# One diffusion step with retention, latent attention and experts on one core: fewer retention state updates, value products placed earlier, input norm placed ahead of the modulation weights

## The chip, the cores and the metric

The kernel runs on one core of a Trainium2 chip, as one program. The metric is the device time of one execution in microseconds (us); of several executions the median is taken. All arithmetic is in 32-bit floats. In the profile every product of the program appears as two matmul records of the same shape (a product of 128x128 by 128x512 is two records of 128x512); a transpose is one record.

## What is computed

640 tokens (128 context tokens and 512 latent tokens, 1024 wide) pass through two layers. Layer 0 mixes tokens by retention in two directions, layer 1 by latent attention; after each comes a mixture of 16 experts. Each norm is scaled and shifted by rows computed from a condition vector.

```
m = silu(cond) @ w_ada + b_ada ; sh1, sc1, g1, sh2, sc2, g2 = split(m)
h = rmsnorm(x, norm1) * (1 + sc1) + sh1
# layer 0, per head (4) and direction (forward, backward), chunks of 128 tokens:
att = (q_c @ k_c.T) * intra
o_c = att @ v_c + (q_c * q_dec) @ s
s   = s * c_dec + (k_c * k_dec).T @ v_c
# layer 1:
cq, ckv, kpe = split(h @ w_in) ; ckv = rmsnorm(ckv, kv_norm)
v = ckv @ w_uv          # values of all keys, 8 heads at once
```

The latent tokens are four chunks that start from a given state; the context tokens are one chunk that starts from zero. The states after the context chunk are outputs; the states after the last latent chunk are not. So a direction has four latent chunks; steps 6 to 9 below compute the outputs of the third and the fourth of each.

## The kernel before

Each engine has its own list of instructions, written out by hand in one function per engine; semaphores tie them. Tokens lie in five tiles of 128; tile 4 (`PT`) is the context. PE means TensorE, DVE VectorE, ACT ScalarE, POOL GpSimd, SP the queue that issues most DMAs.

**Start.** SP issues the small vectors (L559 to L565), then four chunks of `w_ada` of 2 MB each (`load_chunk`, L568), then the five tiles of `x` (L583), then the first weights of head 0 (L568 again). PE multiplies the condition by each chunk (`chunk`, L913), ACT copies the result to `stage` (L1563), PE sums four row groups of it (`chunk_sum`, L939), and ACT copies that to `mod` (L1567). `PRE_ORDER` sets the order of these eight steps. Behind the last one DVE forms `a1` from `mod` (`mod_first`, L1870 and L1871); ACT squares each tile of `x` (`square`, L1559), POOL makes the reciprocal root (`rstd`, L798 and L799), DVE multiplies (`normalise`, L1899), PE transposes eight blocks (`norm_T`, L951), and ACT and DVE each evict half of them with scale and shift into `hT` (`norm_evac`, L1594; `h_evac`, L1890). The first product of head 0 is `P1` (L1058), which reads the ACT half of tiles 0 and 1; then the context's own product (L1074).

**A head of layer 0.** Head 0 is written out, heads 1 to 3 are a loop on every engine. PE computes q, k and v by seven block products on sums of blocks, and the scores of the five chunks (L1155). Then follow ten steps (`STEPS`, a pair of tile and direction each): the product of masked scores and values (L1185), for latent tiles two products of the decayed query and the state (L1193), and, from step 2 to step 9, one update of a state out of `STATES`: two products of 128x512 (L1202), after which two transposes (`k_T`, L1168) fetch the keys of the next update. Behind every step one to three products of the gates (`AFTER_STEP`, L1131) and, in some, a slice of the modulation of a later layer (L923) are placed. DVE takes the statistics of the output (L2099, L2101), updates the state (L2109), scales the transposed keys (`k_decay`, L2048), normalises the output (L2115, which frees bank 5 for the next step), and multiplies by gains and gate. POOL makes the reciprocal roots and the decayed queries (`qdec_mul`, L815).

**Latents of layer 1.** PE computes the latents of each tile (`latent`, L1377 and L1379); POOL, DVE and ACT normalise them; `lat_T` (L1361 to L1365) transposes them into banks 2 and 3; ACT and DVE evict. `lat_T(NT)` does the same for the cached keys. The values of six key tiles (L1400), 24 products into banks 4 to 7, begin when all of that has been evicted; ACT and DVE evict them in turn (L1791, L2363). Then the heads of layer 1 follow (`head_proj`, L1414).

## Time and profile before

| | |
|---|---|
| median of 3 runs | 1804.79 us (1801.92 to 1810.95) |
| the profiled execution's own time | 1819.1 us |
| its span, first to last instruction | 1817.3 us |
| PE busy | 1700.9 us, 94% of the span |
| DVE, ACT, POOL busy | 709.3, 260.7, 180.6 us |
| mean granted clock of TensorE | 0.977 of full speed |

A row of the timeline reads: start, duration from first to last of the merged instructions, engine, line, operation, tiles, sizes, count, and in brackets the idle time ahead and what ended it. The profiled execution is 14.3 us above the median of the runs.

### The profile page before, as it was taken

Reading aid. Unit: us, or ns where it says so; the run is one execution under the profiler, and the core shown is the slowest. Engines: PE = TensorE matmul, PEld = TensorE weight load, DVE = VectorE, ACT = ScalarE, POOL = GpSimd, SP = SyncE. Lnnn points to the kernel's source line nnn. Section 1 sums busy time; section 2 is a strip of 40 time slices with the busy share of each in tenths; the row PEclk is TensorE's granted clock in tenths of the full one; section 3 lists DMA queues with packets and bytes.
Section 4 is the critical chain, followed back from the end, with each engine's and each line's share of the span. In section 5 each row is a group of like instructions: output and inputs, shape, how many; then the busy total and the mean of one; then the engine's idle time right before and its main releaser. Section 6 shows DMA issues by size and latency. Waiting matters only on the chain.

```text
span 1817.3 us, 17218 instructions
## 1 busy us (share of the span) xinstructions
PE 1700.9 (94%) x6322; PEld 953.2 (52%) x6322; DVE 709.3 (39%) x1187; ACT 260.7 (14%) x554; POOL 180.6 (10%) x274
## 2 busy tenths in 40 slices
PE   5999989999899999999898999898999989999995
PEld 2764374643756456644454444354666664544442
DVE  1335533366233553346572322322333333523324
ACT  5100000000000000000121111321323221111111
POOL 1000100011000110001001222110000000012222
PEclk9999999999899999999999999998999999999998
DMA  9432552015410163102766999830000023469994
GB/s 339 172 139 93 177 192 90 0 47 204 178 47 0 67 227 133 46 0 92 256 247 203 342 343 346 253 118 0 24 21 6 7 70 140 167 229 342 344 345 145
DMA packets 159369, 281.38 MB, mean 155 GB/s; under 512 B 11428, under 2 KB 106424, under 8 KB 154184
## 3 DMA queue, kind: packets, MB, share of 16 engines
q1 hardware_dynamic: 144616, 236.39, 37.2%
q0 software_dynamic: 9248, 33.61, 6.9%
q10 hardware_dynamic: 5440, 10.49, 1.6%
q8 instruction: 44, 0.72, 0.2%
q14 instruction: 21, 0.17, 0.0%
HBM read 247.09 MB, written 33.37 MB: 154 GB/s over the span
## 4 chain that ended last, share of the span: by engine, by line
PE 79%; SPq 7%; DMA 5%; DVE 4%; issue 2%; ACT 2%; POOL 0%; ACTq 0%; POOLq 0%; DVEq 0%
PE banks L1058 11%; PE banks L1131 11%; PE banks L1033 8%; PE banks L1293 7%; PE banks L1414 4%; PE banks L1513 4%; SPq L646 4%; PE banks L1127 3%; PE banks L1310 3%; PE banks L1202 3%; PE banks L1193 3%; SPq L647 3%; PE banks L1185 2%; PE banks L1445 2%; DMA wr<-in_moe_w_down 2%
## 5 line engine op out<-in xcount | busy, mean ns | idle before, releaser
L1293 PE MATMUL banks<-wr,arena 128*128 128x512 f32 x512 | 231.4, 606 | 9.6 <-DMA wr<-in_moe_w_down 6.8
L1131 PE MATMUL banks<-wr 128*128 128x512 f32 x432 | 191.4, 592 | 0.0
L1058 PE MATMUL banks<-wr 128*128 128x256 f32 x768 | 173.9, 386 | 10.0 <-issue 8.4
L1058 PEld LDWEIGHTS banks<-wr 128*128 128x128 f32 x768 | 148.1, 194 | 34.5 <-issue 12.5
L1293 PEld LDWEIGHTS banks<-wr,arena 128*128 128x128 f32 x512 | 96.6, 194 | 123.3 <-issue 122.2
L1033 PE MATMUL banks<-wr,arena 128*128 128x512 f32 x320 | 143.6, 604 | 2.1 <-ACT arena L1620 2.1
L1131 PEld LDWEIGHTS banks<-wr 128*128 128x128 f32 x432 | 80.0, 190 | 91.2 <-issue 91.2
L1310 PE MATMUL banks<-wr,arena 128*128 128x512 f32 x256 | 115.4, 593 | 0.9 <-ACT arena L1733 0.9
L1033 PEld LDWEIGHTS banks<-wr,arena 128*128 128x128 f32 x320 | 60.5, 194 | 73.5 <-issue 72.5
L861 POOL DMA_INDIRECT acc_dram<-arena,put_ids x30 | 60.5, 2016 | 264.8 <-DVE arena L2269 264.8
L2254 DVE SCALAR_TENSOR_TENSOR arena<-banks,slot_w,arena 128x256 f32<-128x256 f32 x32 | 15.5, 483 | 182.2 <-ACT arena L1729 182.2
L2269 DVE TENSOR_TENSOR arena<-banks,arena 128x1024 f32<-128x1024 f32 x32 | 39.2, 1225 | 83.4 <-PE banks L1310 83.4
L1310 PEld LDWEIGHTS banks<-wr,arena 128*128 128x128 f32 x256 | 46.3, 190 | 48.3 <-issue 46.9
L1513 PE MATMUL banks<-wr,arena 128*128 128x512 f32 x160 | 69.6, 593 | 0.0
L815 POOL TENSOR_TENSOR arena<-arena 128x256 f32<-128x256 f32 x32 | 23.4, 735 | 377.8 <-DVE arena L2020 377.8
L2099 DVE BATCH_NORM_STATS2 st<-banks 128x6 f32<-128x512 f32 x40 | 28.0, 699 | 82.7 <-PE banks L1193 65.7
L1193 PE MATMUL banks<-arena 128*128 128x512 f32 x128 | 60.1, 592 | 0.0
L1202 PE MATMUL banks<-arena 128*128 128x512 f32 x128 | 60.1, 592 | 0.0
L1970 DVE TENSOR_TENSOR arena<-banks,arena 128x512 f32<-128x512 f32 x40 | 27.6, 691 | 82.5 <-PE banks L1033 82.4
L1127 PE MATMUL banks<-wr 128*128 128x512 f32 x128 | 55.7, 593 | 0.0
L1414 PE MATMUL banks<-arena 128*128 128x512 f32 (+1 forms) x192 | 53.3, 434 | 0.8 <-issue 0.8
L1645 ACT ACTIVATE arena<-arena 128x512 f32<-128x512 f32 x24 | 15.1, 629 | 254.9 <-DVE arena L2079 114.1
(310 smaller groups left out, 2165.7 us busy)
## 6 DMA issues: line engine op xcount, KB each, us to landing
wr<-in_w_ada SPq DMA_DIRECT2D x24, 2048.0 KB, 7.6
wr<-in_moe_w_gate SPq DMA_DIRECT2D x32, 1024.0 KB, 13.4
wr<-in_moe_w_up SPq DMA_DIRECT2D x32, 1024.0 KB, 16.3
wr<-in_moe_w_down SPq DMA_DIRECT2D x32, 1024.0 KB, 15.8
wr<-in_ret_w_in SPq DMA_DIRECT2D x12, 2048.0 KB, 15.9
wr<-in_ret_w_in SPq DMA_DIRECT2D x8, 1024.0 KB, 11.1
wr<-in_ret_w_out SPq DMA_DIRECT2D x4, 2048.0 KB, 7.8
arena<-mod_rows_dram SPq DMA_DIRECT2D x14, 512.0 KB, 6.9
```

The costliest lines, as they stand in the source:

```text
L646: sp.dma_start(gu[:, :, 1, :], w_u[l][e]).then_inc(S(f"w_full{b}"), 16)
L861: g.indirect_dma_start(out=acc[l], out_offset=bass.IndirectOffsetOnAxis(ap=put_ids[:, e:e + 1], axis=0), in_=ysb[:, b, :], in_offset=None, ...
L1033: mm = mmul(bank[6 + hf][:], yT[:, t % 2, j, :], ring(slot)[:, j * D + hf * 512:j * D + hf * 512 + 512], start=(j == 0), stop=(j == 3))
L1058: mm = mmul(dst[:, r * 256:r * 256 + 256], lhs, rhs, start=(start and r == 0 and k == 0), stop=(k == 3), skip_group_check=True)
L1127: mm = mmul(dst, hT[:, k, TS:T], ring8(2 + int(tile))[:, k, :], start=(k == 0), stop=(k == KT - 1))
L1131: mm = mmul(dst, X[X_OF[p]][:, k, cols], W[p][:, k, :], start=(k == 0 and p not in ("P2", "P7", "P3")), stop=(k == 3), skip_group_check=True)
L1193: mm = mmul(bank[5][:], qd[:, u % 2, j, :], St[:, r, j, :], start=False, stop=(j == 1))
L1202: mm = mmul(bank[6 + j][:], kd[:, u % 2, tile_cols(j)], vv[:, STATES[u][0], :], start=True, stop=True)
L1293: mm = mmul(bank[2][:], xgT[:, e.par, k, :], expert_w(e.buf)[0][:, k].rearrange("p g f -> p (g f)"), start=(k == 0), stop=(k == KT - 1))
L1310: mm = mmul(bank[4 + 2 * e.par + hf][:], gactT[:, e.par, j, :], expert_w(e.buf)[1][:, j, hf * 512:hf * 512 + 512], start=(j == 0), stop=(j ...
L1414: mm = mmul(dst, lhs(k), rhs(k), start=(k == 0), stop=(k == nk - 1))
L1513: mm = mmul(bank[4 + hf][:], oTb[:, t % 2, k, :], w_o[:, k, hf * 512:hf * 512 + 512], start=(k == 0), stop=(k == KT - 1))
```

## The change

Three things are changed.

First, each head updates six states instead of eight. `STATES` loses `(3, 0)` and `(1, 1)`. After steps 6 and 7, where these stood, PE now multiplies the keys of that chunk by the queries of the chunk that comes after it (`DIRECT`), DVE scales the scores by both decays into `attm`, and in steps 8 and 9 one more product of these scores and the values stands in for the missing update. The older state is used there, so POOL multiplies the query a second time, by the decay of a chunk.

Second, in layer 1 the values are computed tile by tile by `values(kt)`, the first two ahead of the transposes of the cached keys and of the last latents, in banks 6, 7, 0 and 1; DVE evicts latents 3 before it works on latents 4.

Third, at the start `x` is loaded ahead of the four chunks, its squares stand ahead of the chunk copies on ACT and its first four multiplications ahead of `mod` on DVE. The chunks are taken in the order 0, 2, 1, 3, so that half of the scale and shift (`mod_half`) is there after two of them. The transposes are spread between the chunks, and some small products without a use (`idle_products`) are added on PE.

```diff
-STATES = [(0, 0), (2, 1), (1, 0), (3, 1), (3, 0), (1, 1), (4, 0), (4, 1)]
+STATES = [(0, 0), (2, 1), (1, 0), (3, 1), (4, 0), (4, 1)]
+STATE_AT = {2: 0, 3: 1, 4: 2, 5: 3, 8: 4, 9: 5}
+STATE_FOR = {4: 0, 5: 1, 6: 2, 7: 3, 8: 2, 9: 3}
+DIRECT = {6: (0, 2, 3, 0), 7: (1, 0, 1, 2)}
+DIRECT_FOR = {8: DIRECT[6], 9: DIRECT[7]}
...
+PRE_CHUNK_ORDER = (0, 2, 1, 3)
+FIRST_TILES = (0, 1, 4, 2, 3)
+V_BANK = (6, 7, 0, 1)
...
# SP
-            load_chunk(0, 0, PRE_SLOTS[0])
-            load_chunk(0, 1, PRE_SLOTS[1])
-            load_chunk(0, 2, PRE_SLOTS[2])
-            load_chunk(0, 3, PRE_SLOTS[3])
-            for t in range(NT):
+            for t in FIRST_TILES:
                 src = a["x_prompt"][0] if t == PT else a["x_sample"][0, ORDER[t] * P:(ORDER[t] + 1) * P, :]
                 sp.dma_start(x[:, t, :], src).then_inc(S(f"x_back{t}"), 16)
+            for c in PRE_CHUNK_ORDER:
+                load_chunk(0, c, PRE_SLOTS[c])
...
# POOL, qdec_mul(u)
+                    if u >= 6:
+                        ch.link(ins)
+                        ins = g.tensor_tensor(qd[:, u % 2], qd[:, u % 2], d.unsqueeze(1).to_broadcast([P, 2, P]), ALU.mult)
...
# PE, start
+                idle_products(j % 4, 3)
                 pe.wait_ge(S(f"ring_full{s}"), full[s].next())
...
+            norm_T(0, xn[0], (0, 1))
             for j, (kind, c) in enumerate(PRE_ORDER):
...
+                if j == 5:
+                    pe.wait_ge(S("proj_evac"), 6)
+                    norm_T(0, xn[0], (2,))
             pe.wait_ge(S("proj_evac"), PRE)
-            norm_T(0, xn[0])
-            pe.wait_ge(S("hTa"), NT)
-            pe.wait_ge(S("hTd"), NT)
+            norm_T(0, xn[0], (3, 4))
+            pe.wait_ge(S("hTa"), 3)
+            idle_products(1, 3)
...
# PE, a step of a head
+                        if i in DIRECT_FOR:
+                            pe.wait_ge(S("attm"), h * 6 + i - 3)
+                            mmul(bank[5][:], attm[:, r, at, :], vv[:, tk, :], start=False, stop=False)
                         for j in range(2):
                             mm = mmul(bank[5][:], qd[:, u % 2, j, :], St[:, r, j, :], start=False, stop=(j == 1))
...
-                    if u >= 0:
+                    if i in STATE_AT:
...
+                    if i in DIRECT:
+                        if i == 6:
+                            pe.wait_ge(S("kd_ready"), h * NSS + 5)
+                        else:
+                            pe.wait_ge(S("attm"), h * 6 + 5)
+                        for j in range(2):
+                            mm = mmul(bank[4][:, 2 * P:3 * P], kT[:, j, tile_cols(tk)], qT[:, j, tile_cols(tq)], start=(j == 0), stop=(j == 1))
+                        mm.then_inc(S("att_done"), 1)
...
# PE, layer 1
-            lat_T(NT - 1)
-            lat_T(NT)
-            pe.wait_ge(S("lat_Ta"), NT)
-            pe.wait_ge(S("lat_Td"), NT + 1)
+            values(0)
+            values(1)
+            lat_T(NT)
+            values(2)
+            lat_T(NT - 1)
+            values(3)
+            values(4)
+            values(5)
...
# ACT, start: the squares of all tiles, then
+                for i in {3: (0, 1), 5: (2,), 7: (3, 4)}.get(j, ()):
+                    norm_evac(0, 0, i)
...
# DVE, start
+            for i in range(4):
+                normalise(i)
+            dve.wait_ge(S("proj_evac"), 4)
+            mod_half(0)
+            normalise(4)
             dve.wait_ge(S("proj_evac"), PRE)
-            mod_first(0, 16)
-            normalise(0)
-            normalise(1)
-            for t in range(NT):
-                h_evac(0, 0, t)
+            mod_half(1)
+            for i in range(NT):
+                h_evac(0, 0, i)
...
# DVE, a step of a head, behind the gate's multiplications
+                    if i in DIRECT:
+                        v.scalar_tensor_tensor(out=attm[:, r, at, :], in0=bank[4][:, 2 * P:3 * P], scalar=col(kdec, r), in1=row,
+                                               op0=ALU.mult, op1=ALU.mult).then_inc(S("attm"), 1)
```

At three places the order on PE matters. The first is the start, around the last chunk. Before, in the program's lines of before:

```order
L913 MATMUL banks<-wr,cond 32x512 [waits ring_full1,proj_evac]
L913 MATMUL banks<-wr,cond 32x512 x7
L939 MATMUL banks<-pick,stage 128x2 [waits proj_evac]
L939 MATMUL banks<-pick,stage 128x2 x3
L951 MATMUL banks<-ident,arena 128x128 [waits used,set_a,proj_evac]
L951 MATMUL banks<-ident,arena 128x128 x7
```

With the change (L919 is `idle_products`, L934 `chunk`, L960 `chunk_sum`, L972 `norm_T`, L1084 the product `P1`):

```order
L972 MATMUL banks<-ident,arena 128x128 [waits used,proj_evac]
L972 MATMUL banks<-ident,arena 128x128 x7
L919 MATMUL banks<-ident 128x128 [waits proj_evac]
L919 MATMUL banks<-ident 128x128 x2
L934 MATMUL banks<-wr,cond 32x512 [waits ring_full1]
L934 MATMUL banks<-wr,cond 32x512 x7
L960 MATMUL banks<-pick,stage 128x2 [waits proj_evac]
L960 MATMUL banks<-pick,stage 128x2 x3
L972 MATMUL banks<-ident,arena 128x128 [waits used,proj_evac]
L972 MATMUL banks<-ident,arena 128x128 x7
L972 MATMUL banks<-ident,arena 128x128 [waits hTd,hTa,used]
L972 MATMUL banks<-ident,arena 128x128 x7
```

The transposes of the third tile stand ahead of the last chunk, those of the last two behind it; those of the first two stand ahead of all chunks.

The second place is step 6 of head 0 on PE. Before (L1185 scores by values, L1193 query by state, L1202 update, L1168 transposes of keys, L1131 gate):

```order
L1185 MATMUL banks<-arena 128x512 [waits o_free]
L1193 MATMUL banks<-arena 128x512 [waits S_upd,qd_ready]
L1193 MATMUL banks<-arena 128x512
L1202 MATMUL banks<-arena 128x512 [waits S_upd,kd_ready]
L1202 MATMUL banks<-arena 128x512
L1168 MATMUL banks<-ident,arena 128x128 [waits kd_ready]
L1168 MATMUL banks<-ident,arena 128x128
L1131 MATMUL banks<-wr 128x512 [waits st_d]
```

With the change, in the same order (L1216, L1228, then L1249 the scores of `DIRECT`, L1160 gate):

```order
L1216 MATMUL banks<-arena 128x512 [waits o_free]
L1228 MATMUL banks<-arena 128x512 [waits S_upd,qd_ready]
L1228 MATMUL banks<-arena 128x512
L1249 MATMUL banks<-arena 128x128 [waits kd_ready]
L1249 MATMUL banks<-arena 128x128
L1160 MATMUL banks<-wr 128x512 [waits st_d]
```

Two wide products and two transposes have given way to two narrow products; step 8 has one more wide product.

The third place is the end of the latents on PE. Before it was `lat_T(4)`, `lat_T(5)` and then all values; with the change (L1439 values, L1403 to L1407 `lat_T`):

```order
L1439 MATMUL banks<-wr 128x512 [waits lat_Td]
L1439 MATMUL banks<-wr 128x512 x3
L1439 MATMUL banks<-wr 128x512 [waits lat_Td]
L1439 MATMUL banks<-wr 128x512 x3
L1406 MATMUL banks<-ident,arena 128x128 [waits lat_Td,tab_in]
L1406 MATMUL banks<-ident,arena 128x128
L1407 MATMUL banks<-ident,arena 128x128
L1439 MATMUL banks<-wr 128x512 [waits va,lat_Td]
L1439 MATMUL banks<-wr 128x512
L1439 MATMUL banks<-wr 128x512 [waits vd]
L1439 MATMUL banks<-wr 128x512
L1403 MATMUL banks<-ident,arena 128x128 [waits lat_Td,lat_Ta,kr_ready]
```

Twelve of the 24 products of the values now stand ahead of the transposes of the last latents.

## Rows read from the trace of the kernel before

**Rows 1.** The page: busy time, and the chain that ended last by engine

```profile
PE 1700.9 (94%) x6322; PEld 953.2 (52%) x6322; DVE 709.3 (39%) x1187; ACT 260.7 (14%) x554; POOL 180.6 (10%) x274
PE 79%; SPq 7%; DMA 5%; DVE 4%; issue 2%; ACT 2%; POOL 0%; ACTq 0%; POOLq 0%; DVEq 0%
```

**Rows 2.** Timeline of the start, all engines

```profile
14.41 3.64 PE L913 MATMUL banks<-wr,cond 128*32 128x512 f32 x16 [7.63 <-ACT cond L1542]
14.41 0.19 ACT L1545 ACTIVATE vt<-banks 128x20 f32<-128x20 f32 x1
...
20.57 3.50 PE L913 MATMUL banks<-wr,cond 128*32 128x512 f32 x16
...
25.84 1.92 PE L913 MATMUL banks<-wr,cond 128*32 128x512 f32 x16
...
29.53 1.92 PE L913 MATMUL banks<-wr,cond 128*32 128x512 f32 x16
...
33.40 1.05 ACT L1559 ACTIVATE arena<-x 128x1024 f32<-128x1024 f32 x1
...
36.41 3.64 PE L951 MATMUL banks<-ident,arena 128*128 128x128 f32 x16 [3.12 <-DVE arena L1899]
...
38.38 1.37 DVE L1890 TENSOR_SCALAR wr<-banks,a,mod 128x128 f32<-128x128 f32 x4 [0.65 <-PE banks L951]
...
45.12 1.09 PE L951 MATMUL banks<-ident,arena 128*128 128x128 f32 x8 [1.34 <-DVE arena L1899]
...
47.80 5.34 PE L1058 MATMUL banks<-wr 128*128 128x256 f32 x16 [1.60 <-ACT wr L1594]
...
60.12 3.62 PE L1058 MATMUL banks<-wr 128*128 128x256 f32 x16
```

**Rows 3.** DMA from 20 to 34 us, and SP's issue of the context tile

```profile
21.56 0.64 SPq L583 DMA_DIRECT2D x<-in_x_prompt  x1
...
DMA packets 2224, 5.55 MB, mean 396 GB/s; under 512 B 111, under 2 KB 199, under 8 KB 2224
...
x<-in_x_prompt SPq DMA_DIRECT2D x1, 512.0 KB, 13.2
```

**Rows 4.** Windows: stretch, length, PE busy, granted clock, DMA share, GB/s

```profile
34.00:36.00 2.00, 0.00 (x0) 0.51 1.10 355
```

**Rows 5.** Timeline of PE in head 1: scores, and the update of step 7

```profile
339.05 2.40 PE L1155 MATMUL banks<-arena 128*128 128x128 f32 x20
...
432.89 1.88 PE L1202 MATMUL banks<-arena 128*128 128x512 f32 x4
434.60 0.38 PE L1168 MATMUL banks<-ident,arena 128*128 128x128 f32 x2
434.82 3.60 PE L1131 MATMUL banks<-wr 128*128 128x512 f32 x8
...
445.14 1.13 PE L1185 MATMUL banks<-arena 128*128 128x512 f32 x2 [0.35 <-DVE arena L2115]
```

**Rows 6.** Timeline of DVE in step 7 of head 0

```profile
214.56 0.70 DVE L2099 BATCH_NORM_STATS2 st<-banks 128x6 f32<-128x512 f32 x1 [2.98 <-PE banks L1193]
...
217.87 0.80 DVE L2115 TENSOR_SCALAR arena<-banks,mv,rv 128x512 f32<-128x512 f32 x1
```

**Rows 7.** Timeline at the last latents and the values of layer 1

```profile
1235.74 0.60 PE L1361 MATMUL banks<-ident,arena 128*128 128x128 f32 x4
...
1241.46 1.08 PE L1361 MATMUL banks<-ident,arena 128*128 128x128 f32 x4 [4.79 <-DVE wr L2348]
...
1246.14 22.35 PE L1400 MATMUL banks<-wr 128*128 128x512 f32 x48 [0.81 <-DVE wr L2348]
...
1269.32 8.89 PE L1414 MATMUL banks<-arena 128*128 128x512 f32 x32 [0.83 <-issue]
```

**Rows 8.** Timeline of PE where the loop turns to head 2

```profile
452.91 0.69 PE L1058 MATMUL banks<-wr 128*128 128x256 f32 x2 [2.77 <-issue]
459.21 5.59 PE L1058 MATMUL banks<-wr 128*128 128x256 f32 x14 [5.61 <-issue]
```

More of the change, by code:

```diff
@@ L53 @@
 PRE_CHUNKS = 4
-PRE_ORDER = [(kind, c) for c in range(PRE_CHUNKS) for kind in ("part", "sum")]
+PRE_CHUNK_ORDER = (0, 2, 1, 3)
+PRE_ORDER = [(kind, c) for c in PRE_CHUNK_ORDER for kind in ("part", "sum")]
+FIRST_TILES = (0, 1, 4, 2, 3)
 PRE_SLOTS = (2, 3, 4, 1)
@@ L112, in gate_copy, with swapped @@
     return h * 18 + (7 + GCOPIES.index(name))
+def swapped(n, i):
+    return int(n == 0 and i in (2, 3))
 def slices_done(h):
@@ L899, in _, with idle_products @@
             tpose(bank[7][:, P:P + 20], vraw2[:], ident[0:20, 0:20]).then_inc(S("rows_T"), 1)
+            def idle_products(b, n):
+                for _ in range(n):
+                    mmul(bank[b][:, 0:P], ident[:], ident[:], start=True, stop=True)
             def pre_bank_free(j):
@@ L1069, in products @@
                     pe.wait_ge(S("st_d"), add_no(h, 0, "C21"))
+                if f == 0 and first:
+                    pe.wait_ge(S("hTa"), 4)
+                    pe.wait_ge(S("hTd"), 3)
                 if f == 0:
@@ L1233, in _ @@
             out_proj(RH, 4)
-            def idle_products(b, n):
-                for _ in range(n):
-                    mmul(bank[b][:, 0:P], ident[:], ident[:], start=True, stop=True)
             IDLE_BANK = (7, 4)
@@ L1389, in _, with values @@
                     norm_T(2, xn[1], (t + 2,))
-            lat_T(NT - 1)
-            lat_T(NT)
-            pe.wait_ge(S("lat_Ta"), NT)
-            pe.wait_ge(S("lat_Td"), NT + 1)
-            for kt in range(6):
+            def values(kt):
+                pe.wait_ge(S("lat_Td"), kt + 1)
                 for hf in range(2):
@@ L1865, in cols2, with mod_half @@
                 return ap.unsqueeze(2).to_broadcast([P, n, 2])
+            def mod_half(half):
+                for m0 in (0, 8):
+                    m = mod[:, 0, m0 + 4 * half:m0 + 4 * half + 4, :]
+                    ch.link(v.tensor_tensor(m, m, cols2(vt1[:, m0 + 4 * half:m0 + 4 * half + 4], 4), ALU.add))
+                v.scalar_tensor_tensor(out=a1[:, 0, 4 * half:4 * half + 4], in0=mod[:, 0, 8 + 4 * half:12 + 4 * half, :], scalar=1.0,
+                                       in1=cols2(vt1[:, 96 + 4 * half:100 + 4 * half], 4), op0=ALU.add, op1=ALU.mult)\
+                    .then_inc(S("modA"), 1)
             def mod_first(l, hi):
```

152 lines of the change are left out of this document (87 added, 65 removed).

## The prediction

> **What bounds the kernel now.** I read the page first: PE is busy for 94% of the span and carries 79% of the chain that ended last [rows 1]. So work taken off PE counts almost in full, and work on other engines only where PE waits for it. Next I took the timeline where the change works. At the start PE depends on ACT, DVE and POOL by turns [rows 2]. In the heads it runs without a gap except ahead of step 9 [rows 5]. At the end of the latents of layer 1 it stands still for most of 10 us [rows 7]. DMA is saturated at the start [rows 3], and TensorE's granted clock there is at times 1.2 instead of 2.4 GHz [rows 4]. 0.5% of the median is 9.0 us, about what a measurement of this kernel can tell from no change.
>
> **The values of layer 1.** `lat_T(3)` starts at 1235.74, and a `lat_T` lasts 0.77 us when it runs on (four transposes of 0.60 in the row, then three more), so it is out of the way by 1236.5. Between there and the first product of the heads at 1269.32 lie 32.8 us [rows 7]. What PE must do in it is 24 products. Each is 0.86 us: two of them take 1.71 from 432.89 to 434.60 [rows 5]. That is 20.6; with 0.77 for `lat_T(4)`, about 0.35 for `lat_T(5)`, and the 0.83 ahead of the heads, which stays, 22.5 us. In the new order everything on which the first values wait has been evicted (tiles 0 to 2 long ago). The last latents, which the transposes waited for until 1241.46 with 4.79 us idle, are ready while PE is in its first four and a half microseconds of values; PE needs them only after three tiles of 3.44 and `lat_T(5)`, at 1247.2. The evictions of the values alternate between ACT and DVE, each less than a microsecond against 3.44 a tile, so two banks a side suffice. The 48 records took 22.35, which is 1.7 more than 20.6, since the first ones ran at the lower clock behind the wait; without the wait that goes too. Gain 32.8 - 22.5 = **10.3 us**. Bounds: 4.8 if only the named wait goes and others come in its place, 10.3 if all goes. I take the upper end, since every wait in the new order has over 3 us of slack.
>
> **The heads.** An update costs two wide products, 1.71, and two transposes, 0.22 from 434.60 to 434.82 [rows 5]: 1.93. In its place come two products of 128x128 for the scores, 2.40 / 10 = 0.24 each, 0.48 together [rows 5], and one wide product, 0.86: 1.34. The difference is 0.59, twice a head in four heads: **4.7 us**. DVE loses the update and the scaling of keys and gets one small multiplication from PSUM; all three stand beside PE. The new waits: step 7's scores wait for DVE's copy of step 6's, and step 8 for them. From the statistics at 214.56 to the end of the row that frees the bank, 218.67, DVE takes 4.1 us in a step with an update [rows 6]; without it the bank comes free sooner, and gate products of 3.44 and what else stands there cover it. Three more multiplications follow ahead of the new one, some 2 us, while PE is at the gates and in the next step. POOL's second multiplication is read two steps later. The 0.35 us ahead of step 9 [rows 5] stays, since step 8 keeps its update. Bounds: 0, if the new waits eat it, to 4.7; I take 4.7 as PE has no gap in these steps.
>
> **The start.** Only here does it need a chain. ACT is free at 14.60 [rows 2]. From the start of a square to the transposes it is 36.41 - 33.40 = 3.01 us, so PE begins them at 17.6. Sixteen take 3.64 at the lower clock: until 21.2, then three idle products, six records of 0.2, until 22.4. The first chunk has landed by then: the last byte of the five tiles and four chunks, issued at 21.56, lands 13.2 later, at 34.8; that sum is the same in the new order, and at 396 GB/s a chunk is 5.3 us, so the chunks land at 18.9, 24.2, 29.5 and 34.8 [rows 3]. A chunk's round of product, copy, sum, copy is 20.57 - 14.41 = 6.2 us at the lower and 29.53 - 25.84 = 3.7 at the full clock [rows 2]; idle products add 0.65 or 1.3. Before, the clock came up for the third round, some ten microseconds after PE's first work. I take the lower clock for the first round: 22.4 + 6.2 + 0.65 = 29.2. The second ends at 32.9. Now ACT first evicts tiles 0 and 1 (0.4 for `mod_half`, twice 1.5) and can copy the third chunk only at 36.4, where it would have been ready at 35.5: the third round ends at 38.4. The transposes of the third tile (1.1 [rows 2]) and idle products bring PE to 40.1; the fourth round to 43.8. Then `mod_half` 0.4, DVE's first eviction 1.37, the transposes of the last tile 1.1, idle products 0.65: `P1` starts at 47.4 instead of 47.80. It should then run at the full clock, 3.45 instead of 5.2 (its rows say 3.62 and 5.34, which overlap the next by 0.2). Gain about **2.0 us**. What comes behind it (sums of `hT` on DVE until about 57, the first that PE needs at 61) has its cover. The idle products, 3.3 us in all, are mostly paid here because this is a chain on PE.
>
> Bounds of the start. Were DMA the bound, the last round would start at 34.8 and `P1` at 34.8 + 3.7 + 0.4 + 1.4 + 1.1 + 0.65 = 42.0: a gain of 7.5. Were the lower clock granted all through, three rounds of 7.5 from 22.4, 1.7 of transposes, a round of 6.2, 0.4 + 1.4, 1.7 and 1.3 would put `P1` at 57.6, and 5.2 for it: a loss of 9.8. What I take is nearest to the rows of rounds three and four of before, which ran at the full clock at a like share of work.
>
> The Trainium skill speaks against this part: "TensorE: Matmul & The Clock Gate", section "HAM oscillation — how this bites in real kernels", says that short groups of products with waits for DMA between them each start at the half clock. By it the start would be the loss just worked out instead of the gain. The row at 34 to 36 us, where PE had no work, shows the granted clock down at 0.51 right after PE stopped [rows 4]; rounds with gaps of 0.7 us did not show it.
>
> **Sum.** 10.3 + 4.7 + 2.0 = 17.0 us off the profiled execution's own 1819.1: 1802.1. That execution is 14.3 above the median. At the turn of the loop to head 2 PE stood for 2.77 and 5.61 us with nothing in the profile to wait for, and ran fourteen records at the lower clock, 2.4 us more than at the full one [rows 8, 2]: 10.8 us which the timed runs may lack. The three terms lie elsewhere, so I take them off the median: **1787.8 us**.
>
> **Rivals.**
> 1. DMA bounds the start instead of PE: 7.5 there. For it: the clock may come up earlier, since dense transposes now come first. Time 1782.3.
> 2. Part of the rounds at the lower clock, or the new waits take the heads' gain. Either costs 4 to 6 us: about 1793. For it: PE's work in the rounds is spread thinner than before. Still faster by over 0.5%.
> 3. All rounds at the lower clock: 1787.8 + 2.0 + 9.8 = 1799.6, within 0.5%. This is the page's rule as a mechanism of this kernel. Against it: two rounds ran at the full clock before, and the idle products are dense.
> 4. Slower than before: the stall at the turn of the loop [rows 8] comes at both turns, 21.6 us, in runs that had none before. It decides from 17 us on; the time is 1809.4. For it: the loop's body has another length now and the profile shows one such stall. Against it: the other turn had none, and little in the loop's length changes. The Trainium skill, "Runtime: NRT & Kernel Launch", section "Instruction fetch mechanics", says that a taken branch out of what is prefetched forces a fetch; of the two turns only one agrees.
> 5. The change does not do what it says: the values wait after all for something that I have missed in their new order, and gain only 4.8: 1793.3.
>
> **How the numbers follow.** The forecast (each term within a microsecond or two, 1784 to 1791) has 0.50, rival 1 0.15, rival 2 0.17, rival 3 0.09, rival 4 0.03, rival 5 0.06. Faster by over 0.5% (under 1795.8) are the forecast, rivals 1, 2 and 5, less a little for the spread of the runs: 0.87. Within 0.5%: rival 3 and half of rival 4, with that little: 0.11. Slower: 0.02, rival 4 with a bad start. The range of 8 in 10 takes in rival 1 with the 3 us by which the fastest run lies under the median, 1779, and rivals 2 and 5 with as much on the other side, 1798.
>
> **What would show it.** Values: PE runs on from `lat_T(3)` to the heads in about 22.5 us with no wait over 1 us. Heads: each of the four is 1.2 us shorter, and no wait ahead of steps 7 and 8. Start: `P1` at 47.4, with the full clock. It would be wrong if `P1` starts behind 50, if PE waits for `attm` in steps 7 or 8, or if the first values wait for an eviction.

## The result, and the profile after

The changed kernel took 1794.45 us, median of 7 runs (1786.99 to 1796.72), beside 1810.95 (1801.92 to 1820.58) for the kernel before in as many. The ratio is **0.989, 95% interval 0.9859 to 0.9922**: faster by about 1.1%. Its profiled execution took 1796.69 us, with a span of 1795.1 at a mean granted clock of 0.982 (before 1819.1, 1817.3 and 0.977). Ratios, here and below, are of fast runs, so that one run each of `e2_states` (1826.72) and `e6_no_idle` (1817.81), more than 1.5% above the fastest of its kernel, is not in them.

The spans differ by 22.2 us, and the places where they part are these, each from the starts of the same work in both timelines:

| place | gained, us |
|---|---|
| start, until the context's own product of head 0 (52.98 and 51.03) | 1.95 |
| four heads, 1.24 to 1.26 each | 5.0 |
| turn of the loop to head 2: 14.50 before, 3.45 after, until that head's own context product | 11.05 |
| a longer wait in head 1, and the lower clock behind it | -2.1 |
| between head 3 and `lat_T(3)` | 1.7 |
| `lat_T(3)` to the heads of layer 1: 33.58 and 23.72 | 9.86 |
| from there to the end | -5.2 |

The page of the changed kernel, busy time and chain by engine [as rows 1]:

```profile
PE 1692.6 (94%) x6352; PEld 954.5 (53%) x6352; DVE 702.7 (39%) x1183; ACT 260.8 (15%) x554; POOL 185.5 (10%) x282
PE 81%; DMA 6%; SPq 5%; DVE 4%; issue 2%; ACT 2%; ACTq 0%; POOL 0%; POOLq 0%; DVEq 0%
```

PE is the bound as before. It is busy for only 8 us less, so most of what went was standing still. The timeline of PE at the start [as rows 2]:

```profile
17.56 3.65 PE L972 MATMUL banks<-ident,arena 128*128 128x128 f32 x16 [10.72 <-DVE arena L1961]
21.00 1.49 PE L919 MATMUL banks<-ident 128*128 128x128 f32 x6
22.42 2.10 PE L934 MATMUL banks<-wr,cond 128*32 128x512 f32 x16
...
27.01 1.92 PE L934 MATMUL banks<-wr,cond 128*32 128x512 f32 x16
...
31.47 1.92 PE L934 MATMUL banks<-wr,cond 128*32 128x512 f32 x16
35.28 1.02 PE L960 MATMUL banks<-pick,stage 128*128 128x2 f32 x8 [1.88 <-ACT stage L1611]
36.57 1.97 PE L972 MATMUL banks<-ident,arena 128*128 128x128 f32 x8 [0.27 <-ACT mod L1615]
38.33 1.49 PE L919 MATMUL banks<-ident 128*128 128x128 f32 x6
39.75 1.97 PE L934 MATMUL banks<-wr,cond 128*32 128x512 f32 x16
...
46.00 1.07 PE L972 MATMUL banks<-ident,arena 128*128 128x128 f32 x8 [1.07 <-DVE wr L1951]
...
47.57 3.62 PE L1084 MATMUL banks<-wr 128*128 128x256 f32 x16
```

`P1` starts at 47.57 (forecast 47.4) and at the full clock. Sixteen records of 128x512 of the modulation take 3.64 at the lower clock before [rows 2]; here all four rounds take about 1.92 to 2.10, from the first on. PE then waits 1.88 us ahead of the third sum, because ACT is still at the eviction of the first two tiles. Heads and loop turn, PE's timeline [as rows 5 and 8]:

```profile
250.18 6.06 PE L1084 MATMUL banks<-wr,arena 128*128 128x256 f32 x16 [6.01 <-DVE arena L2067]
...
427.79 1.12 PE L1216 MATMUL banks<-arena 128*128 128x512 f32 x2
...
434.35 1.02 PE L1216 MATMUL banks<-arena 128*128 128x512 f32 x2
...
442.09 1.12 PE L1216 MATMUL banks<-arena 128*128 128x512 f32 x2 [0.35 <-DVE arena L2178]
...
447.34 0.60 PE L952 MATMUL banks<-ident,stage 128*128 128x128 f32 x4
447.78 3.62 PE L1084 MATMUL banks<-wr 128*128 128x256 f32 x16
451.23 7.31 PE L1103 MATMUL banks<-wr 128*128 128x128 f32 x64
```

Steps 7 and 8 of head 1 (427.79 and 434.35) begin without a wait, step 9 keeps its 0.35 (in head 0 it has 1.77 in both kernels). At 447.78 the loop turns to head 2, and the stops of [rows 8] are not there. In head 1 PE waits 6.01 us for the rotated queries (4.37 before), and the sixteen records behind it take 6.06 (5.41 before; 3.62 at the full clock). The end of the latents and the values of layer 1 [as rows 7]:

```profile
1218.17 0.60 PE L1403 MATMUL banks<-ident,arena 128*128 128x128 f32 x4
...
1218.93 7.03 PE L1439 MATMUL banks<-wr 128*128 128x512 f32 x16
1225.80 0.38 PE L1406 MATMUL banks<-ident,arena 128*128 128x128 f32 x2
...
1226.13 3.60 PE L1439 MATMUL banks<-wr 128*128 128x512 f32 x8
1229.57 0.60 PE L1403 MATMUL banks<-ident,arena 128*128 128x128 f32 x4
...
1230.33 10.46 PE L1439 MATMUL banks<-wr 128*128 128x512 f32 x24
1241.89 3.67 PE L1464 MATMUL banks<-arena 128*128 128x512 f32 x8 [1.09 <-DVE wr L2433]
```

Two tiles of values, the transposes of the cached keys, a tile, the last latents' transposes, three tiles: PE runs on for 22 us, and one wait of 1.09 is left.

What came back later did so in good part through the granted clock. These are the last products of the changed kernel and a group ahead of layer 1's output:

```profile
1462.87 1.58 PE L1551 MATMUL banks<-ident,wr 128*128 128x128 f32 x8 [1.64 <-DVE arena L2514]
...
1774.67 6.68 PE L1367 MATMUL banks<-arena 128*128 128x512 f32 x8 [3.21 <-DVE x L2368]
```

The same of the kernel before:

```profile
1490.33 1.06 PE L1501 MATMUL banks<-ident,wr 128*128 128x128 f32 x8 [1.65 <-DVE arena L2436]
...
1799.77 3.70 PE L1327 MATMUL banks<-arena 128*128 128x512 f32 x8 [3.02 <-DVE x L2299]
```

The last records, behind the same kind of wait of 3 us, take 6.68 instead of 3.70: 3.0 of the 5.2 us. The group at 1462.87 takes 0.5 more. The rest lies mostly in a wait for gathered rows ahead of the second mixture of experts, 4.08 us instead of 2.35.

### The profile page after: what moved, and what is told of

Its sections match the earlier page's. It is cut to its first block, busy times and chain, and to the rows that moved or that the text cites. A ratio compares the mean times of both kernels' runs of the same rounds, so it can differ in the third digit from the quotient of the medians.

```text
span 1795.1 us, 17321 instructions
## 1 busy us (share of the span) xinstructions
PE 1692.6 (94%) x6352; PEld 954.5 (53%) x6352; DVE 702.7 (39%) x1183; ACT 260.8 (15%) x554; POOL 185.5 (10%) x282
## 4 chain that ended last, share of the span: by engine, by line
PE 81%; DMA 6%; SPq 5%; DVE 4%; issue 2%; ACT 2%; ACTq 0%; POOL 0%; POOLq 0%; DVEq 0%
PE banks L1160 11%; PE banks L1084 11%; PE banks L1333 8%; PE banks L1059 8%; PE banks L1464 4%; PE banks L1563 4%; PE banks L1350 3%; PE banks L1156 3%; PE banks L1228 3%; DMA wr<-in_moe_w_down 3%; SPq L657 3%; PE banks L1238 2%; PE banks L1216 2%; PE banks L1419 2%; PE banks L1495 2%
## 5 line engine op out<-in xcount | busy, mean ns | idle before, releaser
L1160 PE MATMUL banks<-wr 128*128 128x512 f32 x432 | 191.4, 593 | 0.0
L1084 PE MATMUL banks<-wr 128*128 128x256 f32 x768 | 169.5, 379 | 0.0
L1333 PEld LDWEIGHTS banks<-wr,arena 128*128 128x128 f32 x512 | 96.5, 194 | 123.2 <-issue 121.8
L1084 PEld LDWEIGHTS banks<-wr 128*128 128x128 f32 x768 | 145.3, 190 | 22.7 <-issue 3.7
L1160 PEld LDWEIGHTS banks<-wr 128*128 128x128 f32 x432 | 80.0, 190 | 91.2 <-issue 91.2
L1059 PEld LDWEIGHTS banks<-wr,arena 128*128 128x128 f32 x320 | 60.2, 193 | 72.1 <-issue 71.7
L1350 PEld LDWEIGHTS banks<-wr,arena 128*128 128x128 f32 x256 | 46.3, 190 | 48.3 <-issue 46.9
L1228 PE MATMUL banks<-arena 128*128 128x512 f32 x128 | 60.1, 592 | 0.0
L1563 PEld LDWEIGHTS banks<-wr,arena 128*128 128x128 f32 x160 | 30.5, 194 | 36.9 <-issue 36.9
```

The source lines that it names most:

```text
L1059: mm = mmul(bank[6 + hf][:], yT[:, t % 2, j, :], ring(slot)[:, j * D + hf * 512:j * D + hf * 512 + 512], start=(j == 0), stop=(j == 3))
L1084: mm = mmul(dst[:, r * 256:r * 256 + 256], lhs, rhs, start=(start and r == 0 and k == 0), stop=(k == 3), skip_group_check=True)
L1160: mm = mmul(dst, X[X_OF[p]][:, k, cols], W[p][:, k, :], start=(k == 0 and p not in ("P2", "P7", "P3")), stop=(k == 3), skip_group_check=True)
L1228: mm = mmul(bank[5][:], qd[:, u % 2, j, :], St[:, r, j, :], start=False, stop=(j == 1))
L1333: mm = mmul(bank[2][:], xgT[:, e.par, k, :], expert_w(e.buf)[0][:, k].rearrange("p g f -> p (g f)"), start=(k == 0), stop=(k == KT - 1))
L1350: mm = mmul(bank[4 + 2 * e.par + hf][:], gactT[:, e.par, j, :], expert_w(e.buf)[1][:, j, hf * 512:hf * 512 + 512], start=(j == 0), stop=(j ...
```

## Experiments

Kernels that ran together share the runs of the kernel before; `e1` to `e4`, `e5` to `e8`, `e9` to `e11` and `e12` are such groups. Ratios are to that kernel. The main question came up while they ran: the profile before holds a stop at a loop turn that the one after lacks, so what of the gain is the three edits, and what is that?

**The three parts, each alone.**

`e1_values`, the values' part of the diff on the kernel before:

```diff
-            lat_T(NT - 1)
-            lat_T(NT)
-            pe.wait_ge(S("lat_Ta"), NT)
-            pe.wait_ge(S("lat_Td"), NT + 1)
+            values(0)
+            values(1)
+            lat_T(NT)
+            values(2)
+            lat_T(NT - 1)
+            values(3)
...
```

> The kernel before with the second part alone (values by tile, ahead of the last transposes). Theory A, the sum of the prediction: PE runs on from the transposes of latents 3 to the heads of layer 1 in about 23.7 us instead of 33.6, so the time is 9.9 us under the kernel before, a ratio of 0.9945. Theory B, that the parts do not add up and this one gives back later what it wins (at the experts' weights, which are bound to nothing here): 4 us or less, ratio 0.998.

Measured: 1806.87 us (1794.79 to 1815.6, 12 runs) beside 1809.93 (1806.05 to 1827.51, 29 runs); ratio 0.9965 (0.9934 to 0.9996). The profile has the shorter stretch in full (23.72 us from `lat_T(3)` to the heads), but the interval holds both theories' ratios, 0.9945 and 0.998.

`e2_states`, the heads' part alone:

```diff
-STATES = [(0, 0), (2, 1), (1, 0), (3, 1), (3, 0), (1, 1), (4, 0), (4, 1)]
+STATES = [(0, 0), (2, 1), (1, 0), (3, 1), (4, 0), (4, 1)]
...
```

> The kernel before with the first part alone (six updates a head instead of eight). Theory A: 1.24 us less PE work in each of four heads and no new wait, 5.0 us, ratio 0.9973. Theory B, that the wait for the gate rows in head 1 grows by what head 0 has won, so that one head's gain is lost: 3.7 us, ratio 0.998.

Measured: 1808.1 us (1798.53 to 1826.72, 12 runs); ratio 0.998 (0.995 to 1.0009). Here too the interval holds both theories. The profile, of the run of 1826.72, shows the stop at both turns of the loop: 3.12 and 5.16 us at head 2, 1.76 and 6.23 at head 3.

`e3_start`, the start's part alone:

```diff
-PRE_ORDER = [(kind, c) for c in range(PRE_CHUNKS) for kind in ("part", "sum")]
+PRE_CHUNK_ORDER = (0, 2, 1, 3)
+PRE_ORDER = [(kind, c) for c in PRE_CHUNK_ORDER for kind in ("part", "sum")]
+FIRST_TILES = (0, 1, 4, 2, 3)
...
+                idle_products(j % 4, 3)
...
```

> The kernel before with the third part alone (x first, transposes between the chunks). Theory A: the first product of head 0 starts at 47.6 and runs at the full clock, the time is 2 us under the kernel before, ratio 0.999. Theory B, that the clock at the start varies between executions: the first product starts anywhere between 42 and 55, and the times scatter by several microseconds.

Measured: 1807.86 us (1803.35 to 1811.72, 11 runs); ratio 0.9974 (0.9946 to 1.0003). `P1` starts at 45.1 in its profile, at the full clock, sooner than theory A has it; the interval holds its 0.999, and one profile can't settle theory B. No turn stops, and no run is over 1812, where the kernel before has 9 of 29 over 1817.

`e4_full_again`, the changed kernel once more, unchanged.

> The changed kernel once more, unchanged. Theory A: 1787 to 1797 us, ratio 0.989 to 0.991, the wait in head 1 for the gate rows between 4 and 7 us, and no stall at the turn of the loop. Theory B, that the stall of 8.4 us at the turn of the loop, which the profile of the kernel before showed and that of the changed one did not, comes by chance in either kernel: it may be seen here.

Measured: 1792.34 us (1785.22 to 1796.13, 6 runs); ratio 0.989 (0.9852 to 0.9929). The result repeats to the third digit: theory A, with 5.23 us of wait in head 1 and no stop. `P1` starts at 50.04 here instead of 47.57 and takes 4.71: the same program, another clock from 40 us on. The three parts alone come to 0.35 + 0.2 + 0.26 = 0.8%, together 1.1%.

**Leaving one out, and the places that the profile pointed to.**

`e8_no_states`, the changed kernel with the heads as before:

```diff
-STATES = [(0, 0), (2, 1), (1, 0), (3, 1), (4, 0), (4, 1)]
+STATES = [(0, 0), (2, 1), (1, 0), (3, 1), (3, 0), (1, 1), (4, 0), (4, 1)]
...
```

> The changed kernel without its part on the heads: eight state updates a head as before, the values of layer 1 and the start as changed. Theory A (the heads' part gives its 4.7 us in the presence of the others as well, 1.24 a head by the profiles): ratio to before 0.9915 to 0.992, and profiled heads each 1.24 us longer than in the changed kernel. Theory B (what each part gives is not additive: alone the three came to 0.35, 0.2 and 0.26%, together to 1.1%, because something by chance, as the stop at the loop's turn, is rarer with fewer instructions in the loop's body): ratio 0.994 or more, runs above 1805 among its timed ones, and a stop at a turn in its profile if it falls so.

Measured: 1796.63 us (1793.24 to 1800.55, 6 runs) beside 1811.03 (1803.62 to 1824.11, 17 runs); ratio 0.9917 (0.9884 to 0.995). Theory A: in the presence of the others the heads' part is worth 0.9917 - 0.989 = 0.27%, 4.9 us of 1810. With `e3_start` the values' part comes out too: 0.9974 - 0.9917 = 0.57%, 10.3 us. That leaves 0.26%, 4.7 us, for the start's part. Each of these has an uncertainty of some 0.4%, so that they hit the forecast's terms so closely is partly luck.

`e5_late_wait`, the wait for the first gate row moved behind the loop:

```diff
             def op_evac(h):
+                dve.wait_ge(S("g1_in0"), 32)
                 for t in range(NT):
...
-            dve.wait_ge(S("g1_in0"), 32)
             with dve.Fori(1, RH) as h:
```

> The changed kernel, with DVE's wait for the first gate row moved from ahead of the loop over heads to the eviction of the mixed rows, behind the last head, where the row is first read. Profiled, PE stood 3.8 to 6.0 us in head 1 (at 250.18 in the changed kernel, at 251.76 before) behind DVE's rotation of the queries, and DVE had stood 13.5 us ahead of that rotation for the row's DMA; the 16 matmuls behind PE's stop then ran at 6.06 instead of 3.62. Theory A (DVE stands there for nothing that head 1 needs): no wait over 1 us in head 1 ahead of the sums of its projections, first batch 3.62, head 1 shorter by 6 to 8.5 us; time 1794.5 - 6 to 8 = about 1787, ratio to before 0.986 to 0.985 (0.989 for the changed kernel). Theory B (something else is as late, the evictions of the projections or the rotated keys, so the wait only changes its name): head 1 as long as now, ratio 0.989. Whether the turn of the loop to head 2 shows a stop with nothing to wait for is noted; by chance it may.

Measured: 1789.76 us (1786.54 to 1792.36, 4 runs); ratio 0.9872 (0.983 to 0.9913). DVE in head 1 of the changed kernel, and then PE and DVE there in this one:

```profile
247.64 1.23 DVE L2065 TENSOR_TENSOR wr<-wr 128x1024 f32<-128x1024 f32 x1 [13.48 <-DMA arena<-mod_rows_dram]
```

```profile
244.32 3.62 PE L1084 MATMUL banks<-wr 128*128 128x256 f32 x16
247.78 3.62 PE L1084 MATMUL banks<-wr,arena 128*128 128x256 f32 x16
...
244.52 1.23 DVE L2066 TENSOR_TENSOR wr<-wr 128x1024 f32<-128x1024 f32 x1 [6.59 <-PE banks L1103]
```

Theory A for the place: DVE now waits for PE's product and not for a DMA, PE has no wait at all, and from one head's context product to the next it is 209.21 us instead of 217.82, 8.6 less. The median is 2.6 to 4.7 us lower (than 1792.34 and 1794.45, of other groups), but the ratios' intervals overlap, so that what of it reaches the time is not shown. In the mixture of experts behind the heads PE waits 4.37 us for the gathered rows, where the changed kernel waited 2.60, so 1.8 us are given back there.

`e7_evac_later`, ACT's first evictions later:

```diff
-                for i in {3: (0, 1), 5: (2,), 7: (3, 4)}.get(j, ()):
+                for i in {5: (0, 1, 2), 7: (3, 4)}.get(j, ()):
```

> The changed kernel with ACT's eviction of the first two transposed tiles (2.9 us, behind the copy of the second round's sum) moved behind the copy of the third round's product, together with the third tile's. In the changed kernel PE waits 1.88 us at 35.28 for ACT's copy of the third round's product, because ACT is at those evictions. Theory A (that wait is on the chain to P1): the wait goes, P1 starts 1 to 1.9 us earlier, ratio about 0.988. Theory B (the eviction is only paid later, since P1 needs all tiles): PE waits ahead of P1 or ahead of the third tile's transposes instead, P1 as now, ratio 0.989.

Measured: 1794.27 us (1791.94 to 1797.56, 4 runs); ratio 0.9898 (0.9856 to 0.994), no measurable difference from the changed kernel. The profile shows why:

```profile
34.70 1.03 PE L960 MATMUL banks<-pick,stage 128*128 128x2 f32 x8 [0.81 <-ACT stage L1611]
...
37.93 3.32 PE L934 MATMUL banks<-wr,cond 128*32 128x512 f32 x16
...
48.54 4.85 PE L1084 MATMUL banks<-wr 128*128 128x256 f32 x16
```

The wait went (0.81 instead of 1.88), but the fourth round ran at the lower clock (3.32 against 1.97) and so did part of `P1`. At this start a microsecond of waiting is less than what the clock gives or takes.

`e6_no_idle`, the changed kernel without idle products:

```diff
-                idle_products(j % 4, 3)
...
-            idle_products(1, 3)
```

> The changed kernel without its idle products (identity times identity, three ahead of each of the eight groups of the modulation weights' product and three more ahead of P1, results overwritten). Theory A (they only lengthen a chain on PE): P1 starts 2 to 3.3 us earlier than with them under the same granted clock, so at 44.3 to 48 for the 47.6 and 50.0 of the two profiles of the changed kernel; ratio about 0.987. Theory B (they hold the clock up, and without them the rounds run at the lower clock): a round 6.2 us instead of 3.7, P1 behind 50 and 5.2 us long instead of 3.6, ratio 0.991 or more. If both profiles are mixed, the phase of the clock by chance decides and the ratio stays at 0.989.

Measured: 1809.38 us (1786.83 to 1817.81, 10 runs); ratio 0.9955 (0.9916 to 0.9994). Both theories failed. (The "eight groups" of the expectation are four rounds: 15 idle products in all.) `P1` starts at 47.11, the second and third round run at the full clock, the first and fourth in part at the lower (2.93 and 3.01 where 1.92 is the full clock), so for the start the idle products do little. Yet 0.65%, 12 us, of the gain is gone. The two intervals just overlap, but eight of these ten runs are over 1800, and none of the 21 of the changed kernel, `e5_late_wait` and `e7_evac_later` is over 1797.56. PE at the two turns of the loop:

```profile
447.48 0.60 PE L951 MATMUL banks<-ident,stage 128*128 128x128 f32 x4
450.42 0.48 PE L1082 MATMUL banks<-wr 128*128 128x256 f32 x1 [2.34 <-issue]
456.46 5.21 PE L1082 MATMUL banks<-wr 128*128 128x256 f32 x15 [5.57 <-issue]
...
670.56 0.48 PE L1082 MATMUL banks<-wr 128*128 128x256 f32 x1 [3.12 <-issue]
676.65 6.04 PE L1082 MATMUL banks<-wr 128*128 128x256 f32 x15 [5.61 <-issue]
```

The stop of [rows 8] is here twice, and behind it the lower clock. The DMA view of the whole trace names a queue that carries instructions. First the kernel before, then the changed one, then this one:

```profile
q8 instruction: 44, 0.72, 0.2%
```

```profile
q8 instruction: 36, 0.59, 0.1%
```

```profile
q8 instruction: 53, 0.87, 0.2%
```

A packet is 0.72 MB / 44 = 16.4 KB. The eleven profiles in which no turn stopped (those still to come among them) moved 35 or 36 such packets; the kernel before, with one stop, 8 more; the two with two stops 17 more. They move while the head behind the stop runs: between 430 and 700 us the changed kernel has one, the kernel before nine, this one 14. The view does not say whose instructions they are, but in the changed kernel none begins between 437.6 and 896.6, just while PE is in its loop. So a stop is PE's loop body coming in again, and without a stop the body stays. The Trainium skill, "Runtime: NRT & Kernel Launch", section "Instruction fetch mechanics", states blocks of 16 KiB with 256 instructions each and 2048 instructions for PE; the packet size agrees. By these figures of the Trainium skill, an estimate, the eight packets of one stop hold 2048 instructions. The body has 350 products and 36 transposes: 736 matmul records in the trace, as many weight loads, and some 90 other instructions of PE, about 1565. (The expectations of `e9_small_fill` and `e11_fill_32` were written with four instructions for a transpose too, which has two.) What was left to ask is why 15 products far ahead of the loop matter.

**Time, clock, or place in the program?**

`e9_small_fill` has 15 products of two columns at the head of PE's program, where it waits anyway, in place of the idle ones:

```diff
+            for _ in range(15):
+                mmul(bank[0][:, 0:2], ident[:], ident[:, 0:2], start=True, stop=True)
             pe.wait_ge(S("set_a"), 19)
...
-                idle_products(j % 4, 3)
...
```

> The changed kernel without its 15 idle products, with 15 small ones (identity times its first two columns, result overwritten) at the head of PE's program, in the time in which it waits for the first norm anyway. So PE's loop over heads begins at the same place in its instructions as in the changed kernel, and the chain to P1 holds no idle products. Found so far: without the idle products PE stopped at both turns of the loop for 8 to 9 us with nothing to wait for, and the timed runs went up to 1817.8; in the five profiles of kernels with them (the changed one twice, late_wait, evac_later, no_states) and in the one of the start alone no turn stopped. Theory A (their only worth is that they move the loop's body in PE's instructions, against the pages in which these are fetched): no stop at a turn, P1 at 47 to 48, timed runs within 10 us of each other, median 1790 to 1793, ratio 0.988 or less. Theory B (the idle products work by the clock or by the time at which the loop turns): stops at the turns and a ratio of 0.995, as without them.

Measured: 1792.57 us (1789.44 to 1795.35, 6 runs) beside 1810.72 (1803.57 to 1830.17, 23 runs); ratio 0.991 (0.9876 to 0.9944). PE at its start:

```profile
6.76 6.56 PE L1016 MATMUL banks<-ident 128*128 128x2 f32 x30
17.55 3.65 PE L971 MATMUL banks<-ident,arena 128*128 128x128 f32 x16 [4.23 <-DVE arena L1961]
...
29.38 1.92 PE L933 MATMUL banks<-wr,cond 128*32 128x512 f32 x16 [0.87 <-DMA wr<-in_w_ada]
...
44.90 5.38 PE L1084 MATMUL banks<-wr 128*128 128x256 f32 x16
```

Theory A by the turns and the median; the ratio is 0.991, not 0.988 or less. The small products lie wholly in a wait, the chain has no idle product, and no turn stops. The idle products' worth is their number. `P1` starts at 44.90, earlier than with the idle products (47.57, 50.04), though partly at the lower clock, and the third round waits 0.87 us for its chunk of weights.

`e10_before_fill`, the same 15 lines added to the kernel before and nothing else.

> The kernel before with the same 15 small products at the head of PE's program and nothing else. Theory A (place of the loop's body): no stop at a turn, no timed run above 1812 or so, median 1803 to 1806, ratio 0.996 to 0.998: a third of the change's gain without the change. Theory B (something else of the new start): scatter up to 1820 as before, ratio 1.000, perhaps a stop at a turn.

Measured: 1808.89 us (1806.59 to 1814.58, 12 runs); ratio 0.998 (0.9946 to 1.0014). PE where the loop turns to head 2:

```profile
452.91 0.60 PE L931 MATMUL banks<-ident,stage 128*128 128x128 f32 x4
453.35 3.62 PE L1060 MATMUL banks<-wr 128*128 128x256 f32 x16
```

Theory A in part: no stop, but three runs lie at 1814 to 1815 and the median is above the 1803 to 1806 it named, with no difference from the kernel before that the interval can tell. None of 12 runs is over 1815, where 9 of the 23 of the kernel before beside it are (24 of 83 over all comparisons; were it so here too, none in 12 would have a chance of under 2%). The median moves little, since most runs of the kernel before seem to lack the stop already. Its `P1` started at 50.29, later than 47.80, with the third round at the lower clock too.

`e11_fill_32`, the changed kernel with 32 small products at the head (`range(32)` in the lines above), idle products kept.

> The changed kernel with 32 small products more at the head of PE's program, 128 instructions (two weight loads and two matmuls each), in the time in which PE waits anyway. The loop's body has 386 products, so over 1544 instructions. Theory A (fetched in pages of 256 as the Trainium skill says in Runtime: NRT & Kernel Launch, section Instruction fetch mechanics, with 2048 held: a body of 1544 and more touches seven or eight pages by where it begins, and at eight the page at its head is given up before the turn): with half a page more the body touches eight, the stop comes at one or both turns, median 1800 or more and runs above 1803. Theory B (any products ahead do, or more is better): no stop, median 1792 to 1796.

Measured: 1796.55 us (1787.41 to 1801.72, 12 runs); ratio 0.9914 (0.9886 to 0.9942). No stop, 36 packets: theory A fell as I had put it. Half a block further on is still a good place. All profiles by the number of products and transposes ahead of the loop (453 and 455 are both 843 matmul records, the next two both 873, the last 937):

| products and transposes ahead | kernels | stops at 2 turns | slowest run |
|---|---|---|---|
| 453 | `e2_states`, `e6_no_idle` | 2, 2 | 1826.72, 1817.81 |
| 455 | before, `e1_values` | 1, 0 | 1830.17, 1815.6 |
| 468 | changed (twice), `e5`, `e7`, `e9`, `e12` | 0 in six | 1797.56 |
| 470 | `e3_start`, `e8_no_states`, `e10_before_fill` | 0 in three | 1814.58 |
| 500 | `e11_fill_32` | 0 | 1801.72 |

The good places tried lie within 32 products, 128 instructions, of each other. By the Trainium skill's block of 256, in the section named above, a body of about 1565 instructions would touch seven blocks (the "pages" of the expectation) at 228 of 256 starts and eight at the rest, an estimate; so half a block need not have mattered.

The traces show more of where the edge of a block is. With PE's weight loads, matmuls and other instructions counted in the order of their starts, the branch at the end of the loop's first pass is number 3258 to 3261 in the four kernels with 453 or 455, 3318 to 3321 in the eight with 468 or 470, and 3446 in `e11_fill_32`. An instruction packet begins at number 3262 to 3277 in every profile but that of `e1_values`. So in the good places the packet comes 8 to 29 us ahead of head 2's first product; in the kernel before, `e2_states` and `e6_no_idle` it comes 1.3 to 2.0 us ahead of the stop, beside the branch. In `e1_values`, with the branch at the same place as before, no packet comes there, and no turn stops. This would explain why runs of one kernel fall in two groups, but it is read from 14 profiles, and no run moved the branch by a few instructions to try it.

`e12_best`: `e9_small_fill`, `e5_late_wait` and `e7_evac_later` together, their diffs as above.

> The changed kernel with three edits together: DVE's wait for the gate row late (e5_late_wait), small products at the head of PE's program in place of the idle ones (e9_small_fill), and ACT's eviction of tiles 0 and 1 behind the copy of the third round (e7_evac_later). Profiled, the first took 5.2 to 6.0 us of wait and up to 2.4 us of lower clock out of head 1, the second brought the projections of head 0 from 51.03 to 54.58 (the changed kernel twice) to 50.12, the third took a wait of 1.88 away ahead of the third sum. Theory A (they add, and what they bring early is not given back): head 0's projections done by 49, head 1's wait gone, time 1784 to 1787, ratio 0.985 or less. Theory B (each shift ahead of the heads is given back by the granted clock at other places, as 5 us were behind layer 1's values): 1789 to 1792, no faster than the late wait alone (1789.76).

Measured: **1782.94 us** (1777.8 to 1784.73, 4 runs) beside 1807.49 (1803.81 to 1808.86, 7 runs); ratio 0.9857 (0.9833 to 0.9881). PE at its start:

```profile
29.60 1.92 PE L933 MATMUL banks<-wr,cond 128*32 128x512 f32 x16 [0.99 <-DMA wr<-in_w_ada]
32.32 1.02 PE L959 MATMUL banks<-pick,stage 128*128 128x2 f32 x8 [0.80 <-ACT stage L1611]
...
44.54 5.56 PE L1084 MATMUL banks<-wr 128*128 128x256 f32 x16
```

Theory A by the time (the ratio it named was 0.985 or less). Head 1's wait is gone, `P1` is at 44.54, and the third round waits 0.99 us for its chunk of weights, as it did 0.87 in `e9_small_fill`: DMA has begun to be a bound of the start. The context's own product of head 0 begins at 49.94, a microsecond later than expected, because `P1` ran at the lower clock. It beats both kernels: its slowest run, 1784.73, is under the fastest of 13 of the changed one, 1785.22. How much it gains over that one is less sure, since they ran in different groups: some 10 us by the medians (1792.34 to 1794.45), 6 by the ratios.

## Why the prediction was right, and where it was not

**Direction and size.** The forecast was a gain of 17.0 us; the medians of the first comparison differ by 16.5, and the ratio's interval is 14 to 26 us of 1811. The time, 1787.8, was 6.7 too low. The step behind that is the base: "I take them off the median" used three runs, 1804.79, and with seven the median is 1810.95. The runs of the kernel before fall in two groups, about 1802 to 1815 and 1817 to 1830, most likely since the turn of the loop stops in some (one execution was profiled, 1819.1, with one stop). Three runs had no high one. The range held the time.

That the size came out so close is partly luck. In the profiles the three terms came to 16.8 us, but 7.3 were lost again in head 1 and behind the values, 1.7 won ahead of `lat_T(3)`, and 11.05 came from the turn of the loop, which the sum had left out.

**Values of layer 1, 10.3.** Profiled 9.86; by the runs 10.3. "PE runs on from `lat_T(3)` to the heads in about 22.5 us": from the end of `lat_T(3)` it is 23.0, mostly since the wait ahead of the heads, now for DVE's last eviction, is 1.09 instead of 0.83. "No wait over 1 us" missed by that 1.09. Rival 5 is out.

**Heads, 4.7.** Profiled 5.0 (1.24 to 1.26 a head against 1.18); by the runs 4.9. No wait ahead of steps 7 and 8, 0.35 ahead of step 9, as said. The half of rival 2 on new waits is out.

**Start, 2.0.** The milestones came as worked out: 22.4 for the first chunk (22.42), 40.1 for the fourth round (39.75), `P1` at 47.4 (47.57) with the full clock, gain 1.95. Two errors on the way cancelled: the first round ran at the full clock already, so that the second began 2.2 us sooner than taken, and the idle products and transposes around 37 ran at the lower. But the hit says little. `P1` began at 50.04 when the same kernel was profiled again, and the context's product at 48.56 to 54.80 in the seven profiles with this start and its idle products. Their mean is 52.3, that of the four with the old start (52.77 to 55.53) 53.9: the order is worth 1.6 us, with a scatter of 3 by the clock. Rival 3, the lower clock in every round, was in no profile of the new start: rounds with gaps of 0.7 to 1.9 us ran at the full clock. The Trainium skill, "TensorE: Matmul & The Clock Gate", section "HAM oscillation — how this bites in real kernels", has its rule from a kernel that waits 3 to 5 us for DMA between its groups, longer than any gap between these rounds, so the prediction stretched it. Rival 1 was not reached: PE waited for ACT, not for DMA, until `e9_small_fill` and `e12_best` shortened its chain.

**What the start's part also did.** "The idle products, 3.3 us in all, are mostly paid here" is the step that failed in substance: it counted what they cost on the chain and took their place in the program for nothing. They also move PE's loop to where its turns never stopped in ten profiles, and without them 12 us of the gain were gone. That is what the forecast had set apart as "10.8 us which the timed runs may lack". Of 83 timed runs of the kernel before 59 are under 1815, where they seem to have lacked it, and 24 above. Rival 4 looked at the right stop with the wrong sign: the change took the stop away instead of doubling it. That place, and not time or clock, does it is shown by `e6_no_idle` against `e9_small_fill` (the same program without and with 15 small products at its head) and supported by `e10_before_fill`; that it is the branch beside a block's edge is read from the packets' times, and not tried.

**Not foreseen.** Head 1's wait for the rotated queries is in the trace of the kernel before (4.37), and its cause is a wait of DVE for a gate row that is read much later. An earlier start of the heads made it longer, 2.1 us given back; `e5_late_wait` showed the cause. Another 5.2 us behind the values went mostly to the lower clock and to the gather, none of it where the change is.

## What to carry to other kernels

Before crediting an edit with a gain, ask what else it moves: 15 overwritten products looked like help for the clock and were worth some 12 us through the place of a loop some hundreds of products behind them. A stop "for nothing that the profile shows" at a loop's turn is checked in the instruction queue's packet count, and cured by filler in an idle stretch. A wait that stands ahead of a loop for a tile that is read behind it should move to its reader. Take the base of a prediction from enough runs to see whether they fall in groups.

## What the runs showed of the hardware

- A turn of PE's loop (about 1565 instructions) costs nothing, or 7.9 to 8.7 us of stop and some 2 to 3 us at the lower clock, with 8 to 9 instruction packets of 16.4 KB more. With 453 or 455 products and transposes ahead of it 5 of 8 profiled turns stopped, with 468 to 500 none of 20.
- A product with two columns costs as much time as one with 128: 30 records of 128x2 in `e9_small_fill` took 6.56 us, 0.22 each, and 16 of 128x128 at the lower clock 3.65, 0.23 each.
- The granted clock in a chain of short work is not repeatable: the fourth round at the start took 1.97 and 3.03 us in the two profiles of the changed kernel, and its last eight records 6.68 and 5.40 behind a wait of a little over 3 us (3.70 in the kernel before).
